# All retention queries and keys join the conditioned front of a one-core encoder layer, summed per job into SBUF

## The reference, cut to what matters

```
mod = silu(c) @ w_ada + b_ada            # (2048) @ (2048, 6 * 2048)
sh1, sc1, gt1, sh2, sc2, gt2 = split(mod, 6)
h = rms_norm(x, g_mix) * (1 + sc1) + sh1
rq, rk, rv, rg, aq, ak, av = split(h @ w_in + b_in)
ret = retention(rq, rk, rv, rg)          # 4 heads of 256, rotated q and k
att = window_sink_attention(aq, ak, av)  # 16 query, 2 key/value heads of 64
x = x + gt1 * (concat(ret, att) @ w_out)
x = x + gt2 * conv_glu(rms_norm(x, g_ffn) * (1 + sc2) + sh2)
y = rms_norm(x, g_final) * (1 + f_scale) + f_shift   # silu(c) @ w_final_ada
```

## Time and profile before

| | us |
|---|---|
| median of three runs | 1212.85 |
| span of the profiled execution, first to last instruction | 1212.2 |
| TensorE busy | 1176.3 |
| VectorE busy | 876.4 |
| ScalarE busy | 654.7 |

### The profile page before, as it was taken

How to read it: one execution, slowest core, us unless ns; L and a number is a source line. 1 busy time by engine, 2 the same in 40 slices (tenths; PEclk the granted TensorE clock), 3 DMA queues, 4 the chain that set the end, 5 groups by cost and what they waited for, 6 DMA issues and landing times.

```text
span 1212.2 us, 19582 instructions
## 1 busy us (share of the span) xinstructions
PE 1176.3 (97%) x6728; PEld 979.7 (81%) x6728; DVE 876.4 (72%) x1065; ACT 654.7 (54%) x950; POOL 179.7 (15%) x307
## 2 busy tenths in 40 slices
PE   5799999999999999999999999999999999999995
PEld 1466999977888788888888888888888877888784
DVE  2333557888799887887887887877665666898886
ACT  3233457364345448565565666656655555555652
POOL 6443202221211110110111010000000001120101
PEclk9999999999999999999999999999999999999998
DMA  9999989999798984888888878785555557896841
GB/s 353 391 390 387 332 343 356 371 378 336 267 338 321 332 290 165 298 285 277 287 281 280 290 270 291 271 290 177 188 193 180 198 180 284 288 355 251 311 175 69
DMA packets 164852, 342.97 MB, mean 283 GB/s; under 512 B 10078, under 2 KB 102848, under 8 KB 164160
## 3 DMA queue, kind: packets, MB, share of 16 engines
q1 hardware_dynamic: 126832, 206.13, 48.5%
q0 software_dynamic: 37536, 134.30, 29.7%
q10 hardware_dynamic: 432, 1.84, 0.4%
HBM read 340.14 MB, written 2.10 MB: 282 GB/s over the span
## 4 chain that ended last, share of the span: by engine, by line
PE 92%; DMA 4%; DVE 2%; issue 1%; POOL 1%; ACT 0%; DVEq 0%; POOLq 0%; ACTq 0%
PE ps L1375 27%; PE ps L1351 15%; PE ps L1352 15%; PE ps L1353 15%; PE ps L1380 14%; DMA ada_raw<-in_w_ada 3%; PE ps L1459 2%; DMA arena<-in_w_ada 1%; DVE xb L1149 1%; DVE arena L1147 0%; PE ps L1606 0%; PE ps L1440 0%; PE ps L1711 0%; PE ps L1586 0%; PE ps L1569 0%
## 5 line engine op out<-in xcount | busy, mean ns | idle before, releaser
L555 ACT ACTIVATE whi<-raw 128x1024 fp32r<-128x1024 f32 x256 | 271.6, 1062 | 286.4 <-PE ps L1380 180.6
L896 DVE TENSOR_TENSOR wlo<-raw,whi 128x1024 fp32r<-128x1024 f32 x256 | 311.8, 1222 | 104.0 <-ACT whi L555 104.0
L1375 PE MATMUL ps<-hh,whi 128*128 128x512 f32 x1408 | 353.0, 392 | 0.3 <-issue 0.3
L1375 PEld LDWEIGHTS ps<-hh,whi 128*128 128x128 f32 x1408 | 253.2, 189 | 45.8 <-issue 0.5
L1351 PE MATMUL ps<-whi,hh 128*128 128x512 f32 x608 | 241.4, 397 | 0.3 <-ACT gate L754 0.3
L1353 PE MATMUL ps<-whi,hh 128*128 128x512 f32 x608 | 236.9, 390 | 0.0
L1352 PE MATMUL ps<-wlo,hh 128*128 128x512 f32 x608 | 236.6, 389 | 0.0
L901 DVE SCALAR_TENSOR_TENSOR acc<-ada_raw,c_act,acc 128x1024 f32<-128x1024 f32 (+1 forms) x176 | 224.8, 1278 | 5.7 <-DMA ada_raw<-in_w_ada 5.1
L548 ACT ACTIVATE whi<-raw 128x1024 fp32r<-128x1024 f32 x124 | 130.8, 1060 | 169.7 <-PE ps L1353 144.9
L891 DVE TENSOR_TENSOR wlo<-raw,whi 128x1024 fp32r<-128x1024 f32 x124 | 151.3, 1222 | 92.5 <-ACT whi L548 92.4
L1380 PEld LDWEIGHTS ps<-hh,wlo 128*128 128x128 f32 x1408 | 192.1, 190 | 13.7
(11 more groups left out here) (141 smaller groups left out, 787.5 us busy)
## 6 DMA issues: line engine op xcount, KB each, us to landing
raw<-in_w_up SPq DMA_DIRECT2D x176, 512.0 KB, 4.4
ada_raw<-in_w_ada POOLq DMA_DIRECT2D x144, 512.0 KB, 6.9
raw<-in_w_down SPq DMA_DIRECT2D x44, 1024.0 KB, 6.2
ada_raw<-in_w_final_ada POOLq DMA_DIRECT2D x64, 512.0 KB, 5.3
raw<-in_w_in SPq DMA_DIRECT2D x28, 1024.0 KB, 8.1
arena<-in_w_ada POOLq DMA_DIRECT2D x48, 512.0 KB, 9.5
raw<-in_w_out SPq DMA_DIRECT2D x16, 1024.0 KB, 8.1
raw<-in_w_in SPq DMA_DIRECT2D x28, 512.0 KB, 8.0
```

The costliest lines, as they stand in the source:

```text
L555: nc.scalar.activation(whi[:, i % RING, :], raw_of(step0 + i), ACT.Copy).then_inc(hi_ready, 1)
L896: nc.vector.tensor_tensor(wlo[:, i % RING, :], raw_of(step0 + i), whi[:, i % RING, :], ALU.subtract).then_inc(lo_ready, 1)
L1375: nc.tensor.matmul(bank_of(m), whi[:, slot, tile(m, j)], hh[:, k0 + j, :, :].rearrange("p i s -> p (i s)"), start=start and j == 0, stop=F ...
```

## The change

- `STEP_RQB` is gone. Steps 0 to 51 now hold all retention queries and keys. Job 0 is loaded and summed in two parts (`first_units`, `first_pair`, `first_sums`), each giving two k-tiles; so there are five stages of h, of 2, 2, 4, 4 and 4 k-tiles (`STAGE_K`).
- In each stage the queries and keys of all four heads are multiplied (`two_heads`, four groups of two heads) into banks 5, 6 and in part 7 and 4, evicted after each group, and summed in SBUF (`first_heads` on ScalarE and VectorE, `add_heads` on VectorE). The order of steps on TensorE in stages 2 and 3 is, four times, one step of attention queries and two of heads, with a pair between them, eight pairs in all; the sum of the job after the fourth step of queries.
- From job 2 on pairs use four slots (two pairs ahead); the other four hold units of jobs 5 and on, which begin in stage 2 (`UNITS`).
- Each early step has a semaphore of its own (`front_in`).
- Values and gates follow at once (p 10 and p 26 of now 42), retention's scores at p 27 to 30 and values at p 35 to 41 through one bank.

```diff
-FRONT = 6
-FRONT_START = (0, FRONT, 2 * FRONT, 3 * FRONT + 2)
+STAGE_K = ((0, 1), (2, 3), (4, 5, 6, 7), (8, 9, 10, 11), (12, 13, 14, 15))
+AQ_STEPS = (0, 2, 6, 8, 12, 15, 18, 21, 24, 27, 30, 33, 38, 39, 40, 41)
+AK_STEPS = (36, 37, 42, 43)
+SPILL_STEPS = (((1,), (3,), (4,), (5,)), ((7,), (9,), (10,), (11,)),
+               ((13, 14), (16, 17), (19, 20), (22, 23)), ((25, 26), (28, 29), (31, 32), (34, 35)),
+               ((44, 45), (46, 47), (48, 49), (50, 51)))
+STEP_P0 = 42
+STEP_RV, STEP_RG, STEP_WO0, STEP_WO1, STEP_UP = (52 + KT * i for i in range(5))
-PAIR_AT = (3, 7, 11, 15, 19, 23, 27, 31)
+PAIR_AT = (0, 3, 6, 9, 12, 15, 18, 21)
+UNIT_STEPS = ((16, 18, 19, 21), (28, 30, 31, 33, 34), range(38, 48), (49, 51, 53, 54), range(55, 66), (66, 66, 67, 67, 68, 69),
+              (72, 72, 73, 74, 75, 76, 77, 77, 78, 79, 79, 80, 81, 82, 83), (84, 87, 87, 88), range(91, 98),
+              (100, 101, 102, 103, 104, 105, 107, 108, 109), (111, 112, 113, 114, 115))
```

On SP:

```diff
+            after_unit(0, 6)
+            load_queries(0)
+            after_unit(0, 7)
+            load_heads(0, 0)
+            after_unit(0, 8)
+            load_queries(1)
```

On GpSimd:

```diff
+            def first_units(part):
+                for i in range(2 * RING):
+                    if i % 2 == 0 and part:
+                        pool.wait_ge(ada_pe, i // 2 + 1)
+                    k, first = 4 * (i // 2), i % 2 * D + 256 * part
+                    pool.dma_start(ada_of_slot(i).rearrange("p (k n) -> p k n", k=4),
+                                   ada_k[:, k:k + 4, first:first + 256]).then_inc(ada_in[i], 16)
+            first_units(0)
+            next_acc(0)
+            first_units(1)
+            next_acc(1)
+            with pool.Fori(0, 2) as turn:
+                eight_units(1, turn)
+            next_acc(2)
+            next_acc(3)
+            pair_units(2, 0)
+            pair_units(2, 1)
+            next_acc(4)
+            for n in range(4):
+                dve_unit(n)
+            for n in range(2, PAIRS):
+                pair_units(2, n)
...
+            for n in range(2, PAIRS):
+                pair_units(3, n)
+                if n in (3, 5, 7):
+                    dve_unit(8 + (n - 3) // 2)
```

On ScalarE:

```diff
             hi_group(0, 0, 3)
-            for job in range(4):
...
+            stage_in(0)
+            hi_group(0, 3, 5)
+            first_heads(0, 0)
+            hi_group(0, 5, 7)
+            first_heads(1, 0)
+            stage_in(1)
+            hi_group(0, 7, 14)
+            stage_in(2)
```

On VectorE:

```diff
             for step in range(3):
                 lo(step)
-            for job in range(4):
-                pe_rows(job)
...
+            first_rows(0)
+            mod_cols(0, FIRST_BANKS[0], 0, 0)
+            for k in STAGE_K[0]:
+                h_lo(k, 0)
...
+            def add_heads(stage, group):
+                which, h0 = group // 2, group % 2 * 2
+                dve.wait_ge(step_done, SPILL_STEPS[stage][group][-1] + 1)
+                for h in (h0, h0 + 1):
...
+                    nc.vector.tensor_tensor(part if stage < 4 else qk_flat[which][:, h, :],
+                                            ps[:, SPILL_BANK[stage][4 * which + h], :], part, ALU.add).then_inc(spill, 1)
...
+                elif p == 28:
+                    token_values()
                 elif p == 29:
                     maxima(1)
...
+                if 31 <= p < 35:
+                    ret_decay(p - 31)
```

On TensorE:

```diff
+            pe.wait_ge(ones_ready, 6)
+            first_pair(0, 0)
+            first_pair(0, 1)
...
+            first_pair(0, 2)
+            first_pair(0, 3)
...
+            first_sums(0)
...
+            att_queries(0)
+            first_pair(1, 0)
+            two_heads(0, 0, 0)
+            first_pair(1, 1)
+            att_queries(1)
+            first_pair(1, 2)
+            two_heads(0, 1, 0)
+            first_pair(1, 3)
+            two_heads(0, 2, 0)
+            first_sums(1)
+            two_heads(0, 3, 0)
...
+            for n in range(4, PAIRS):
+                ada_pair(1, n)
+            sum_columns(1, ADA_BANK[1], 0)
+            two_heads(1, 3, 0)
+            for stage in (2, 3):
+                for group in range(4):
+                    att_queries(STAGE_K[stage][group])
+                    if group < 3:
+                        ada_pair(stage, 3 * group)
+                    else:
+                        sum_columns(stage, ADA_BANK[stage], 0)
+                    for i in range(2):
+                        two_heads(stage, group, i)
+                        if group < 2 or group + i == 2:
+                            ada_pair(stage, 3 * group + 1 + i)
...
             def ret_scores(h):
+                if h:
+                    pe.wait_ge(st_ready, 2 * h)
+                else:
+                    pe.wait_ge(v_ready, 4)
+                    pe.wait_ge(rot_done, 12)
...
+            rv_free = [(k2_ready, 5), (spill, 30), (spill, 31), (spill, 32)]
+            rg_free = [(mod_ready, 7), (v_ready, 1), (v_ready, 2), (v_ready, 3)]
...
+                elif 27 <= p < 31:
+                    ret_scores(p - 27)
+                elif p in (35, 37, 39, 41):
+                    ret_values((p - 35) // 2)
```

More of the change, by code:

```diff
@@ L243, in raw_value @@
         def raw_value(step):
-            chunks = range(raw_slot(step), step // 2 + 1, RING)
-            return sum(32 if STEP_UP <= 2 * chunk < STEP_DN or 2 * chunk < STEP_RQB else 16 for chunk in chunks)
+            chunks = [n for n in range(raw_slot(step), step // 2 + 1, RING) if 2 * n >= STEP_RV]
+            return sum(32 if STEP_UP <= 2 * n < STEP_DN else 16 for n in chunks)
         def rows_before(job):
@@ new lines, in _ @@
+            mod_cols(0, FIRST_BANKS[0], 0, 0)
+            for k in STAGE_K[0]:
+                h_lo(k, 0)
+            for step in range(3, 7):
+                lo(step)
+            first_heads(0)
+            first_rows(1)
+            mod_cols(0, FIRST_BANKS[1], 0, 1)
+            for k in STAGE_K[1]:
+                h_lo(k, 0)
+            first_heads(1)
+            for step in range(7, 11):
+                lo(step)
+            add_heads(1, 0)
+            lo(11)
+            lo(12)
+            add_heads(1, 1)
@@ L989, in values_out @@
+            for step in range(38, STEP_P0):
+                lo_units(step)
             def values_out():
@@ L1156, in _ @@
                     residual((i - 4) // 2, 0, x1_part, GT1_READY, res1_tmp)
-                if units < 5 * KT and i not in (6, 10):
-                    unit(units)
-                    units += 1
+                for _ in range(UNITS.count(STEP_WO1 + i)):
+                    ada(JOB_DVE + units[0] // KT, units[0] % KT)
+                    units[0] += 1
             def token_part(t, done):
@@ L1384, in tokens @@
             def tokens(slot, k, start, bank0, order=range(4), free=None):
+                banks = bank0 if type(bank0) is tuple else range(bank0, bank0 + 4)
                 for n in order:
@@ L1561, in att_scores @@
+            keys_values(0)
+            keys_values(1)
+            for k in STAGE_K[4]:
+                att_queries(k)
             def att_scores(batch, j):
@@ L1682, in _ @@
                 pe.wait_ge(lo_ready, STEP_WO0 + i + 1)
-                tokens(i % RING, (8 + i) % KT, i == 0, 0, free=None if i else [(g_raw, b + 1) for b in range(4)])
+                tokens(i % RING, (8 + i) % KT, i == 0, 0, free=None if i else wo_free)
                 if i in (5, 6):
```

613 lines of the change are left out of this document (346 added, 267 removed).

## The result

The changed kernel takes 1261.14 us (median of 4 runs, 1259.65 to 1263.04) against 1212.73 for the kernel before (4 runs, 1211.64 to 1215.37): ratio 1.040, with a 95% interval of 1.0388 to 1.0413. The profiled execution has a span of 1258.0 us. Forecast were 1219 and a range up to 1228: the direction was right, the size was not (48 us instead of 6), and the time lies outside the range.

A forecast was written before the change was run, and what follows sets the result against it. Transfers were taken to set the front's speed, with TensorE full after it. From 1212.2, minus 5.0 and 2.0 gives 1205.2 us; plus 13.6 gives a 1218.8 span, put at 1219; range 1203 to 1228.

The forecast's parts named there:

- Point 1: Waits between jobs on TensorE: 5.0 us of idle time, all removed at best.
- Point 2: The start: first step at 37.7 us, 9.6 earlier, but pairs move behind it; gained 2.0 us (0 to 4).
- Point 3: TensorE's clock, lowered by little work before the first step: 1.5 us added (0 to 3).
- Point 4: Job 1's last four pairs together, its sum right behind: VectorE's part and handovers show, 1.1 us (0.7 to 2).
- point 8: VectorE's added additions, 26 us, mostly beside steps that leave it free; first values step waits 0.5 us (0 to 3).
- Rival (e): GpSimd's queue: pair 2,0 is 6 us late behind a wait for biases; 1225 us, chance 0.02 alone.
- Points 5 and 6: Stages 2 and 3: transfers fall short of TensorE's time, 3.8 us (0 to 18) and 2.4 us (0 to 10).
- Point 7: Job 4's pairs at every third step: transfers need 76 us against TensorE's 74; 1.0 us taken (0 to 4).
- Point 9: Retention through one bank: TensorE waits for decay behind VectorE's queue, 3.0 us (0 to 6).
- (a): Stores suffice: filled slots and raw steps ahead carry stages 2 and 3; faster, at 1206 us, chance 0.25.
- (b): Even: half of the added waits, job waits go and as much returns at pairs and retention; 1212 us, chance 0.25.
- Rival (d): Thinner supply: transfers at 349 GB/s, a unit takes 1.50 us; 1232 us, chance 0.05.

The follow-up runs named there:

- e3: Changed kernel with stage 0's modulation ahead of all conversions on ScalarE and VectorE; 1247.97 us.
- e13: e10 plus e5, six pair slots, scores ahead of additions, two retention banks; VectorE's first nine units load 64 of 1024 columns, leaving work out; 1219.17 us.
- e4_all: Changed kernel with e3's edit, three SyncE waits on job 1's units removed, and stage 1's additions moved ahead of conversions on VectorE; 1240.57 us.
- e17: e13's base, nothing left out: VectorE's units of steps 16 to 33 go behind step 33, asked for behind job 3's pairs; 1222.69 us, ratio 1.0085.
- e5: e4_all with the conversion of step 13 behind job 1's sum, stage 2's modulation and add_heads(1, 3), on both engines; 1239.45 us.
- e9: e4_all without SyncE's last wait on a unit of job 1, after_unit(1, 15); 1239.32 us.
- e10: e9 with the second half's four pairs of job 0 ahead of step 0 on TensorE; 1236.32 us.
- e15: e13's base with job 0's second-half pairs back between the first steps and add_heads(4, 3) ahead of step 54's conversion; 1230.34 us, ratio 1.0135.

## Why the prediction was wrong, step by step

Point 1 (waits between jobs go): right in kind. Step 6 starts 2.96 us behind step 5 instead of 9.35, though part of that is work that moved.

Point 2 (step 0 at 37.7): measured 43.16. The order of events was the predicted one, conversions of steps 0 to 2 first; the raw tile of step 2 was issued at 23.39, where I had put it at 23.7, but took 12.7 us to land instead of 7.7, at 36.1 instead of 31.4, and from there it took 7.0 us instead of 6.3. **What failed is that I priced this order and did not question what it costs.** The first half's pairs were done at 23.8, and e3 shows that a start at 32 us was there for the exchange of a few lines.

Point 3 (slow clock 1.5, 0 to 3): the granted clock was 0.50 in 30:40, the lower of its two levels; from 24 to 38 us TensorE had been busy 1.07 us. Step 0 with its pair took 6.14 us instead of 4.07: 2.1. Within its bounds.

Point 4 (job 1's sum exposed 1.1): 1.79 us, a size. Its surroundings were the fault.

**Between points 4 and 8 stands the step that failed most: the price of the additions in point 8.** Point 8 says of the 32 additions that "most lie beside steps that leave it free: 3.67 of 10 busy". I priced them as work for an idle engine. They are reads that free banks, in a queue in which conversions wait for transfers. From step 6 to step 12 the changed kernel takes 43.3 us; six steps, eight pairs and a shown sum are 17.3 + 9.5 + 2.2 = 29.0 by my own prices. That leaves 14.4 us, of which 13.7 are TensorE's two waits for these additions, and which no term or rival held. Rival (e) came nearest, with GpSimd's queue, at 0.02.

Points 5 and 6 (stages 2 and 3, 3.8 and 2.4): the mechanism was right, the size half: TensorE waited 7.9 us for units from 112 to 165 us and 4.6 from 165 to 240, 12.5 against 6.2 and within the bounds 0 to 28. e13 confirms the term's own ground, VectorE's units ahead of the pairs (8.3 us in its setting). The transfers moved 390 to 397 GB/s in 110:130, 150:160 and 180:190, and 245 to 348 in the other windows of ten from 130 to 180. I had counted on slots filled ahead. That too little was asked for in time is likely, but the ring of stage 1 is not the reason: with it open, in e4_all, TensorE waited 13.2 us for pairs from 40 to 240 us, against 12.4 in the changed kernel.

Point 7 (job 4's pairs 1.0): 1.6. Right.

Point 8, the rest (values' first step 0.5, 0 to 3): 1.5. But the additions of stage 4 ahead of the scores, 5.2 us in 4 waits, were not seen, though I wrote that VectorE has 3.7 to 4.7 us of work per step there; I looked for what is late in sum, not for what stands behind what.

Point 9 (one bank for retention 3.0, 0 to 6): 2.8 us of waits, and 3.8 us less between steps 70 and 72 with two banks. Right.

The sum: by the prediction's terms step 44 starts at 218.6 - 7.0 (points 1, 2) - 9.6 (work that moves behind it) + 8.8 (points 3 to 6) = 210.8, and from there to step 79 it is 121.45 + 9.6 + 4.8 (points 7 to 9) = 135.9 us. The changed kernel has 240.4 and 144.6. So 30 of the 38 us missed lie in the front, 9 behind it. e17 has 210.2 and 137.7, so most of the miss was order and slots and not an unknown cost of the parts. That its sum comes so near the prediction's is partly luck: step 0 starts at 40.4 and not 37.7, the 3.0 us of point 9 are gone by the second bank, and the 4.0 us of waits for scores stood in no term. Rivals (a) and (b), a time at or below the kernel before, came out in no full version run here; moved work costs nothing by itself, but the front never won more than it had handed on.

Rival (d), a thinner supply of 349 GB/s at some price per byte, was not the cause: in 100:110 the transfers moved 402 GB/s, and 394 and 390 in the two windows behind. The Trainium skill's figure of about 358 GB/s per core ("DMA: Bandwidth & Descriptors", "Where 436 GB/s comes from") is passed again by the row of 100:110, as by the earlier trace rows.

What stays open: why steps 36 of e4, e5, e9 and e10 agree within 1.3 us in spite of different fronts was not settled beyond the part that e13 shows; why the units landed late in e15 is open; and whether attention's first batch could stand ahead of step 44 in the new order was not tried.

## What to carry to other kernels

When an operation is put into an engine's queue, ask first what stands ahead of it that waits for a transfer, and who needs its result: a read that frees a PSUM bank, put behind a conversion whose tile is late, holds TensorE for the whole landing, however idle its engine is (10.3 us here, on an engine that was busy 3.65 of 10). A gate that delays one transfer until another has landed is safe only while the second does not depend on the work that the first feeds; follow slot, unit, gate, conversion and bank once around. And a single page of shares will not show it: the starts of the steps in two traces, side by side, did, once the work that had moved from one side of a step to the other was counted.

## What the runs showed that was not expected

While the first half's units came in (in pieces of 256 columns, 1 KB a row), the DMA engines were as busy as before and moved less. The window 10:25 of the kernel before, then of the changed one:

```profile
10.00:25.00 15.00, 12.66 (x61) 4.56 (x62) 4.52 (x7) 6.11 (x9) 10.22 (x14) 1.00 1.03 391
```

```profile
10.00:25.00 15.00, 12.38 (x101) 7.70 (x101) 4.43 (x7) 6.60 (x9) 8.16 (x11) 1.00 1.03 350
```

A share of 1.03 in both, 391 and 350 GB/s. It is not the other queue: GpSimd's own packets in this window, before and after (packets, MB, share of the engines' time), are

```profile
q0 software_dynamic: 1492, 5.21, 91.5%
```

```profile
q0 software_dynamic: 1473, 5.12, 100.3%
```

About as many packets of about the same size took a tenth longer. In all it is 0.6 MB in 15 us, or 1.6 us of transfers. It may be part of why the raw tile of step 2 was late; no run changed the pieces, so that they are the cause is not shown.
